# Dense passes over the second expert table in a Trainium2 decoder layer: one pass for tiles 3 and 5, or two passes for tiles 2, 3 and 5, 6

## What is computed

```python
idx = take_along_axis(cand_i, top_pos)        # (C, 8, 16): the experts picked
g = softmax(top_s)
u = peer_u[idx]                               # first table, one row per pick
a = gelu(einsum('cd,chkd->chk', xc, u))
v = peer_v[idx]                               # second table, one row per pick
out = einsum('chk,chkd->cd', g * a, v)        # weighted sum of the rows
```

## Time and profile before

| | before |
|---|---|
| time, median of 3 runs | 3650.37 us (3649.11 to 3658.34) |
| span of the profiled execution | 3659.0 us |
| TensorE busy | 3082.9 us, 84% |
| VectorE busy | 2704.0 us, 74% |
| GpSimd busy | 2336.6 us, 64% |
| ScalarE busy | 921.9 us, 25% |
| DMA | 1259.50 MB, mean 344 GB/s |
| mean granted TensorE clock | 0.902 of full |

### The profile page before, as it was taken

The page is one execution under the profiler, slowest core; times in us unless marked ns, Lnnn a source line. Parts: engine busy times, 40 slices in busy tenths (PEclk is TensorE's granted clock), DMA queues, the critical chain, the costliest instruction groups (busy, mean ns, idle before and its releaser), DMA issues.

```text
span 3659.0 us, 32490 instructions
## 1 busy us (share of the span) xinstructions
PE 3082.9 (84%) x8982; PEld 1564.7 (43%) x8982; DVE 2704.0 (74%) x6074; ACT 921.9 (25%) x2252; POOL 2336.6 (64%) x1940
## 2 busy tenths in 40 slices
PE   7897697899986987777987986458999998889998
PEld 4664343467553433333433431134543445544333
DVE  2218877787679988878998899977975579955555
ACT  2112232422223321153222121134410015510000
POOL 0006543677556766878776667786877668877775
PEclk9898897778998998887998998779999999899999
DMA  6359986899999999998999999998999999899999
GB/s 152 105 173 364 356 276 199 303 376 376 346 357 375 361 378 312 333 345 316 402 388 396 403 355 370 347 358 320 337 409 409 409 408 371 311 377 409 409 409 369
DMA packets 425721, 1259.50 MB, mean 344 GB/s; under 512 B 61000, under 2 KB 106728, under 8 KB 425531
## 3 DMA queue, kind: packets, MB, share of 16 engines
q0 software_dynamic: 276480, 1006.76, 72.6%
q1 hardware_dynamic: 141125, 244.91, 19.8%
q10 hardware_dynamic: 7936, 5.77, 0.5%
HBM read 1229.04 MB, written 28.25 MB: 344 GB/s over the span
## 4 chain that ended last, share of the span: by engine, by line
PE 35%; DVE 15%; DMA 14%; POOL 13%; issue 10%; SPq 2%; ACT 2%; another core or an unknown queue 1%; ACTq 0%; DVEq 0%; POOLq 0%
DMA vbuf<-in_peer_v_dram,idx 9%; PE pY L1667 8%; POOL ubuf L942 8%; PE pb L1538 6%; POOL vbuf L954 5%; DVE ubuf L2327 4%; PE pb L1640 4%; PE pb L1292 3%; PE pb L1556 3%; DVE acc L2348 2%; PE pb L1627 2%; DMA ubuf<-in_peer_u_dram,idx 1%; PE pb L1584 1%; DMA R<-c_scratch 1%; PE pb L1511 1%
## 5 line engine op out<-in xcount | busy, mean ns | idle before, releaser
L942 POOL DMA_INDIRECT ubuf<-in_peer_u_dram,idx x1088 | 1367.0, 1256 | 917.9 <-DVE dots L2327 320.2
L2327 DVE CUSTOM_DVE_ANT_0 ubuf<-ubuf,hnf 128x1024 f32<-128x1024 f32 x1088 | 1314.4, 1220 | 331.6 <-DMA ubuf<-in_peer_u_dram,idx 288.7
L1667 PE MATMUL pY<-vbuf,dg 128*128 128x512 f32 (+1 forms) x1956 | 1039.1, 662 | 242.5 <-DMA vbuf<-in_peer_v_dram,idx 139.8
L954 POOL DMA_INDIRECT vbuf<-in_peer_v_dram,idx x832 | 966.7, 1162 | 390.5 <-issue 230.8
L1667 PEld LDWEIGHTS pY<-vbuf,dg 128*128 128x128 f32 (+1 forms) x1956 | 366.9, 200 | 740.0 <-issue 508.5
L2348 DVE SCALAR_TENSOR_TENSOR acc<-vbuf,gw,acc 128x1024 f32<-128x1024 f32 x343 | 439.9, 1282 | 57.4 <-DMA vbuf<-in_peer_v_dram,idx 48.4
L1640 PE MATMUL pb<-R 128*128 128x512 f32 x1024 | 460.3, 593 | 1.2 <-issue 0.7
L1538 PE MATMUL pb<-R 128*128 128x256 f32 (+2 forms) x1152 | 361.7, 475 | 8.9 <-DMA R<-in_w_in_dram 4.4
L1929 ACT ACTIVATE gel<-dots 128x4 f32<-128x4 f32 x272 | 55.5, 204 | 1076.3 <-DVE dots L2327 863.5
L1640 PEld LDWEIGHTS pb<-R 128*128 128x128 f32 x1024 | 194.6, 191 | 245.2 <-issue 243.9
L1538 PEld LDWEIGHTS pb<-R 128*128 128x128 f32 x1152 | 221.6, 193 | 145.7 <-issue 93.0
(11 more groups left out here) (252 smaller groups left out, 2717.7 us busy)
## 6 DMA issues: line engine op xcount, KB each, us to landing
R<-in_peer_v_dram SPq DMA_DIRECT2D x128, 512.0 KB
R<-in_w_in_dram SPq DMA_DIRECT2D x12, 2048.0 KB
R<-in_w_in_dram SPq DMA_DIRECT2D x24, 1024.0 KB
R<-in_w_query_dram SPq DMA_DIRECT2D x24, 1024.0 KB
ubuf<-in_peer_u_dram,idx POOLq DMA_INDIRECT x1088
vbuf<-in_peer_v_dram,idx POOLq DMA_INDIRECT x832
R<-in_w_out_dram SPq DMA_DIRECT2D x12, 1024.0 KB
R<-in_x_prompt_dram SPq DMA_DIRECT2D x16, 512.0 KB, 8.8
```

Source lines behind the costliest of these rows:

```text
L942: pool.indirect_dma_start(out=ubuf[:, n % RING, :], out_offset=None, in_=peer_u[0], in_offset=bass.IndirectOffsetOnAxis(ap=idx[:, t % NI, ...
L954: pool.indirect_dma_start(out=vbuf[:, v % RING, :], out_offset=None, in_=peer_v[0], in_offset=bass.IndirectOffsetOnAxis(ap=idx[:, t % NI, ...
L1667: ins = pe.matmul(pY[0:rows, half, :], dg[:, CPE[m] % RDG, 0:rows], vbuf[:, v % RING, half * 512:(half + 1) * 512], start=first, stop=(t ! ...
L2327: dve.tensor_tensor_reduce(ubuf[:, n % RING, :], ubuf[:, n % RING, :], hnf[:, par, :], 1.0, 0.0, ALU.mult, ALU.add, dots[:, q % 2, n % GRP ...
```

## The change

`PASSES` becomes `[(2, 3), (5, 6)]`: tiles 2 and 3 get their second-table sum from a dense pass at picks 596 to 836 and tiles 5 and 6 from one at picks 836 to 1086. Only tiles 0, 1, 4, 7 and 8 are left with V gathers, 576 in all. `TAKEN` and `OWN` are new: no V gather in picks 0 to 127; by stretches there are

| picks | V gathers before (TensorE, VectorE) | after (TensorE, VectorE) |
|---|---|---|
| 0 to 63 | 33 (29, 4) | 0 |
| 64 to 127 | 29 (21, 8) | 0 |
| 128 to 255 | 42 (3, 39) | 78 (10, 68) |
| 256 to 383 | 131 (76, 55) | 76 (63, 13) |
| 384 to 511 | 96 (18, 78) | 64 (26, 38) |
| 512 to 575 | 48 (10, 38) | 38 (11, 27) |
| 576 to 831 | 191 (153, 38) | 64 (3, 61) |
| from 832 on | 262 (179, 83) | 256 (104, 152) |

The dense work now lies so:

| pass, half | pieces in picks | table steps in picks |
|---|---|---|
| first, first | 597 to 636 | 637 to 714 |
| first, second | 715 to 754 | 755 to 832 |
| second, first | 837 to 877 | 879 to 959 |
| second, second | 960 to 1000 | 1002 to 1082 |

The slots of the groups end at picks 59, 274 and 600, and the choices move by a few picks (tile 7's to 750 to 833, tile 8's to 883 to 932). The semaphore counts of the pass are worked out for two passes (`turned`, `piece`, `evicted`, `turn_out`), the stores of the dense tiles get a semaphore of their own (`yd_out`), which the second pass's loads 1 and 2 wait for, and three small constant semaphores become two.

```diff
-    PASSES = [(3, 5)]
+    PASSES = [(2, 3), (5, 6)]
+    PASS_AT = [596, 836, 1086]
...
+    GROUP_AT = [(0, 59), (53, 274), (284, 600)]
+    CHOOSE_AT = {1: (58, 126), 3: (282, 352), 4: (410, 492), 6: (608, 690), 7: (748, 836), 8: (882, 934)}
...
-            spread(slots, START[FIRST[g - 1]] + (50 if g == 1 else 25), START[FIRST[g]] + 24)
-    for t in range(NT + 1):
-        if t not in FIRST:
-            spread(choose(t), START[t - 1] + (52 if t == 1 else 26), ENDS[t - 1] - 20)
-    for ps, pair in enumerate(PASSES):
-        spread(dense(ps), ENDS[pair[1]] + 4, NPK - 6 if ps + 1 == len(PASSES) else ENDS[PASSES[ps + 1][1]] + 4)
+            spread(slots, *GROUP_AT[g])
+    for t in CHOOSE_AT:
+        spread(choose(t), *CHOOSE_AT[t])
+    for ps in range(len(PASSES)):
+        spread(dense(ps), PASS_AT[ps], PASS_AT[ps + 1])
...
-    TAKEN = [18, 15, 15, 14, 10, 10, 12, 10, 32, 32, 32, 35, 27, 27, 25, 17, 17, 31, 32, 16, 16, 5, 26, 32, 32, 32, 32, 32, 32,
-             32, 32, 32, 32, 32, 6]
-    OWN = [0, 0, 3, 9, 7, 10, 12, 10, 6, 18, 16, 15, 26, 18, 17, 17, 16, 22, 9, 0, 0, 0, 4, 3, 10, 12, 11, 12, 4, 9, 11, 11,
-           12, 11, 2]
+    TAKEN = [0, 0, 0, 0, 19, 13, 19, 27, 27, 13, 17, 19, 23, 19, 2, 20, 18, 10, 14, 6, 14, 16, 6, 14, 14, 0, 4, 30, 34, 26, 36, 36, 24, 32, 36]
+    OWN = [0, 0, 0, 0, 19, 13, 19, 17, 1, 2, 6, 4, 14, 8, 0, 16, 14, 6, 5, 5, 14, 16, 6, 14, 14, 0, 2, 15, 21, 15, 21, 20, 22, 17, 12]
...
-                    if b >= 3:
-                        sp.wait_ge(dm_d, NK * ps + b - 2)
+                    if u >= VRR:
+                        if b in (1, 2):
+                            sp.wait_ge(yd_out, 32 * ps)
+                        else:
+                            sp.wait_ge(dm_d, NK * ps + (b - 2 if b else 0))
```

More of the change, by code:

```diff
@@ L180, in build, with turned, piece, evicted @@
     OHR, VRR = 3, 3
-    NT_D = 2 * len(PASSES)
+    def turned(ps, j):
+        return ps * (2 + 2 * NPIECE) + j + 1
+    def piece(o):
+        return 2 * (o // (2 * NPIECE) + 1) + o + 1
+    def evicted(o):
+        return 2 * (o // (2 * NEV) + 1) + o + 1
+    def turn_out(ps, j):
+        return ps * (2 + 2 * NEV) + j + 1
     RINGW, NWO = 4, 4
@@ L804, in build @@
         DV0 = 2 * NB * P
-        assert len(PASSES) == 1 and VRR <= RINGW
+        assert VRR <= RINGW
         vr = [R[:, DV0 + k * D:DV0 + (k + 1) * D] for k in range(VRR)]
@@ L837, in build @@
         skb = [pb[:, 5, :], pY[:, 0, :], pY[:, 1, :], pb[:, 5, :]]
-        c_sel, c_hr, c_one, gain_in, ones_out, sk_in, skT_d, skT_c = (
-            sem(x) for x in ("c_sel", "c_hr", "c_one", "gain_in", "ones_out", "sk_in", "skT_d", "skT_c"))
+        c_sel, c_dve, gain_in, ones_out, sk_in, skT_d, skT_c = (
+            sem(x) for x in ("c_sel", "c_dve", "gain_in", "ones_out", "sk_in", "skT_d", "skT_c"))
         dve_s, act_s = sem("dve_s"), sem("act_s")
@@ L889, in build @@
         oh_d, ow_d, wm_d, we_d, dm_d, dy_d = (sem(x) for x in ("oh_d", "ow_d", "wm_d", "we_d", "dm_d", "dy_d"))
+        yd_out = sem("yd_out")
         def run_slot(stages, slot):
@@ L1207, in vl @@
                     u = ps * (NK + 2) + b
-                    if b == 0:
+                    if u == 0:
                         sp.wait_ge(q_d, PH * GN)
@@ L1223, in ys @@
                     sp.wait_ge(dy_d, 2 * ps + j + 1)
-                    sp.dma_start(yp_out[blk(t) * P:(blk(t) + 1) * P, :], vr[u % VRR]).then_inc(y_out[j], 16)
+                    sp.dma_start(yp_out[blk(t) * P:(blk(t) + 1) * P, :], vr[u % VRR]).then_inc(yd_out, 16)
                 def picks(n):
@@ L1242, in _ @@
                 for par in range(2):
-                    sp.wait_ge(y_out[par], 16 * (y_upto(par) + len(PASSES)))
+                    sp.wait_ge(y_out[par], 16 * y_upto(par))
                     sp.wait_ge(k_out[par], 16 * upto(par, NT))
                     sp.wait_ge(v_out[par], 16 * (upto(par, NT) + upto_p(par, NT)))
+                sp.wait_ge(yd_out, 32 * len(PASSES))
                 sp.wait_ge(pool_out, 16 * (4 + NSEQ))
@@ L1622, in wm @@
                     pe.wait_ge(ow_d, o + 1)
-                    if p % 2 == 0:
-                        pe.wait_ge(we_d, NT_D + o // 2)
+                    if p == 0 and half == 0:
+                        pe.wait_ge(we_d, turn_out(ps, 1))
+                    elif p % 2 == 0:
+                        pe.wait_ge(we_d, evicted(o // 2 - 1))
                     for a in range(NTOK):
@@ L1897, in d_cp @@
                     k = 2 * ps + j
-                    act.wait_ge(wm_d, k + 1)
+                    act.wait_ge(wm_d, turned(ps, j))
+                    if ps and j == 0:
+                        act.wait_ge(oh_d, piece(2 * NPIECE * ps - 1))
                     act.activation(dT[:, j].rearrange("p x t -> p (x t)"), pb[:, 4, 0:3 * P], ACT.Copy).then_inc(we_d, 1)
@@ L1904, in ow @@
                     j, t0 = divmod(p * NTOK, P)
-                    act.wait_ge(oh_d, NT_D + o + 1)
+                    act.wait_ge(oh_d, piece(o))
                     for a in range(NTOK):
@@ L1912, in we @@
                     o = (2 * ps + half) * NEV + e
-                    act.wait_ge(wm_d, NT_D + 2 * o + 2)
+                    act.wait_ge(wm_d, piece(2 * o + 1))
                     if o == 0:
@@ L2371, in d_ab @@
                             dve.wait_ge(q_st[par], 16 * QST[LASTG, PH - 2 + par])
+                    if ps and j == 0:
+                        dve.wait_ge(wm_d, piece(2 * NPIECE * ps - 1))
                     dve.tensor_scalar(ints[:, 0, :], num, 7, None, ALU.logical_shift_right)
@@ L2380, in oh @@
                     if p == 0 and half == 0:
-                        dve.wait_ge(we_d, NT_D)
+                        dve.wait_ge(we_d, turn_out(ps, 1))
                     if o >= OHR:
-                        dve.wait_ge(wm_d, NT_D + o - OHR + 1)
+                        dve.wait_ge(wm_d, piece(o - OHR))
                     shape = [P, NTOK, NK]
```

24 lines of the change are left out of this document (13 added, 11 removed).

## The result

The two passes are slower: 3862.97 us (3860.11 to 3866.35) against 3649.74 us, ratio 1.057, 95% interval 1.055 to 1.060. The forecast was 3696 us, and 3785 at most. The direction was right and the size wrong: +213 us where +46 was forecast. The profiled execution has a span of 3861.3 us (3659.0 before) and a mean granted clock of 0.858 (0.902).

What follows compares the result with a forecast made beforehand. No single bound: the largest of the TensorE, VectorE, GpSimd and DMA loads bounds each stretch. Picks 0 to 575 -90, 576 to 831 +79, the rest +57 sum to +46 us, 3696 us; range 3590 to 3785.

Steps and rivals of the forecast that it cites:

- The four loads: Every stretch: the largest of TensorE, VectorE, GpSimd with issue time and DMA bytes at 409 GB/s bounds it.
- The cut from -114 to -90 us: Picks 0 to 575: stretch gains sum to -114 us, taken as -90 because a sum of averages is too kind.
- the table steps: Picks 637 to 1082: four phases of 64 steps, 230, 230, 292 and 291 us, by TensorE and DMA loads.
- The step that failed: Four stretches of 64 pieces: VectorE's load bounds them, 137, 124, 134 and 139 us.
- The prediction's own sign: In the pieces VectorE should be the busiest engine, near 95%.
- the balance of the trade itself: Whole kernel: DMA 164 us and GpSimd 384 us less, TensorE 70 us and VectorE 140 us more.
- Relief beyond the loads: Rival 1, first 576 picks: overhead of 141 us shrinks too, 3600 us in all; chance 0.24.
- The ring of three table buffers: Rival 3, picks 637 to 832: ring too short, steps 4.1 us apart, +64 us, 3760 us; chance 0.06.
- The poor pattern of the table stream: Table-step phases: a table tile costs twice 1.28 us of DMA, +282 us, 3978 us; chance 0.02.
- rival 4: Table tiles at twice 1.28 us: step phases 306, 277, 371 and 371 us, 3978 us in all; chance 0.02.

Runs made afterwards that it cites:

- y3: Changed kernel with one added 128x512 matmul behind each of the 64 pieces of the first pass's first half: 3831.70 us, ratio 1.046.
- y1: Changed kernel with each eviction one slot later and two PSUM banks in turn in each pass's first half: 3736.12 us, ratio 1.022.

## Why the prediction was wrong, step by step

- **What bounds the kernel now.** The four loads were right, and so was the method in the phases other than the pieces: picks 0 to 575 came out at 1724 us for 1725, the table steps at 1039 for 1043 in sum, with steps 3.64 and 3.77 us apart in the first pass, just above the 3.5 to 3.6 of the forecast. The cut from -114 to -90 us was a guess, and that it came out within 1 us is luck. That the changed kernel's table steps are bound by TensorE at full clock in the first pass and together with the DMA in the second is in the rows above (227 of 233 us; 283 of 286 at a DMA share of 1.02).
- **The step that failed** is the one in which "VectorE has 40 x 1.14 = 46 for dots, 64 x 0.94 = 60 ..." bounds the pieces and "ScalarE, 86 us, and TensorE lie below". VectorE's load was sized well (546 us busy for 534), but being the largest load is not being the bound. The prediction's own sign was there: VectorE was to be near 95% busy in the pieces, and it was 79% (546 of 695 us). The overlap was wrong: each engine's load was taken as free to run beside the others, while eviction, one piece's scalings and a pair's products stand in a row, 5.31 us a pair at the lower clock. In the first pass this gives 2 x 32 x 5.31 = 340 us against 336 measured and 261 forecast. In the second pass, 359 us for 273, the same order stands among V buffers, and how much each link holds there was not measured. Before, 64 pieces had 61 picks and 200 us; with 64 in 40 picks the loop came out from under the other loads.
- **The clock** was not in my sum for the pieces: I had TensorE's products at 1.0 us a piece, and in the first pass they took 1.84. It fell to 0.53 in the first pass, where stretches of pieces had 0.86 to 0.89; as I read it, because the wide V buffers that stood between the products were gone from there (3 and none in the two stretches, at 0.53 and 0.52; 21 and 17 in the second pass, at 0.70 and 0.67). It made the products' link 3.67 us instead of 2.0. By y3 this is at least 20 us of the first stretch's miss of 34; for the other stretches it was not measured. Without it the loop, 3.70 us a pair, would have stayed below VectorE's load in the first pass. So a sum that had added up the row with products of 1.0 us a piece would have missed it as well.
- **Where all of it went.** Forecast +46, chain and clock +161 in the trace: 3705 + 161 is 3866 for a span of 3861. With the chain loosened (y1) the kernel is +79 and its pieces take 574 us, 40 above the 534; 79 - 40 = +39 is close to the +46 of the forecast. This speaks for the balance of the trade itself, DMA saved against TensorE and VectorE spent.
- **The rivals.** Relief beyond the loads did not come: picks 256 to 575 fell by 96 us, 97 forecast, 150 wanted. The ring of three table buffers was no bound: over 256 steps TensorE's weight loads on L1664 waited 73.0 us for the table and its matmuls 13.6. The poor pattern of the table stream did not show either: the 64 steps of 3088 to 3374 us took 286 us, where rival 4 had 371, and the DMA moved 404 GB/s. The rule of the Trainium skill on rows 512 KiB apart ("DMA: Bandwidth & Descriptors", section "Latency and other measured facts") does not describe this stream beside gathers: the Trainium skill has it for tiles of 16 KiB a row moved by themselves, and these have 4 KB. None of my rivals was the one that happened; the range ended at 3785 because no case had a chain in the pieces.
- **A version that beats both** was not found. The late eviction with two banks and added matmuls gives 3722 us; even with all pieces at VectorE's load the sum from y1 leads to 3736 - 40 = 3696, an estimate, above the 3650 of one pass.

## What to carry to other kernels

When a schedule packs a step closer together that several engines share, follow one result through all of them in the order of each engine's program, add up what stands in a row, and multiply it by the count. Only then compare it with the engines' loads: the larger of the two is the bound. Don't take a distance from a trace for this row without looking at what fills it; in the trace before, 5.35 us was TensorE's own work. Work the row out at both clock levels of TensorE, 3.70 and 5.31 us here, and ask whether the edit takes away the work that kept the clock up. In a hand-ordered program, an instruction that waits for the engine downstream belongs behind the one that this engine needs next; one slot was worth 113 us here.

## What was not expected of the hardware

TensorE ran at a granted clock of 0.53, nearly all of it at the lower level, while it was 74% busy (127 of 171 us) with matmuls 64 columns wide, and its longest wait for a scaling there was 2.8 us. Sixty-four more matmuls of 512 columns in the same stretch brought the clock to 0.99, with TensorE busy for 129 of 150 us. In the kernel before, 2272 to 2402 us had a clock of 0.75 with TensorE busy for only 62 of 130 us. So the busy share in the profile did not tell which clock would be granted.
